# Even attention in 32-row tiles with two score sets, transposes as ordinary matmuls, out panels beside the head norm, rotation inside the projections

## The chip, the cores and the metric

The kernel runs on one core of one Trainium2 chip. The metric is the device time of one execution in microseconds (us); the median of the timed runs counts. PE is the matmul engine, DVE the vector engine, ACT the scalar engine, POOL the general one, SP the engine that issues most DMAs.

## The reference

Two model blocks over 512 tokens of width 1024 (and 256 context tokens), all in float32. The change touches the first mixer of the first block, the even one:

```
px, pc = hx @ w_in, hc @ w_in                    # x and context, 8 parts of 512 columns
qa, ka = axial_rope(q part), axial_rope(k part)  # x tokens only; 8 heads, 2 maps each, 32 wide
s = einsum(q, k) * 32**-0.5                      # per head and map m = 0, 1
p = softmax(s); a = p[m=0] - lam * p[m=1]        # lam = exp(..) - exp(..) + lam_init
o = einsum(a, v)                                 # v 64 wide
out_a = rms_norm(o over the head's 64) * subln * (1 - lam_init) * silu(ga)
out_b = short_conv(bb, cb, ub) * silu(gb)
x = x + g_x * rms_norm(concat(out_a, out_b) @ w_out, norm_post)   # context alike
```

x queries see 768 keys (256 context, 512 x), context queries the 256 context keys. The odd mixer, the sliding-window attention, the SGU and two FFNs follow and are not touched.

## The kernel before

Activations lie feature-major: partitions are features, columns are tokens (TX = 512 x tokens, TC = 256 context tokens, TA = 768). Weights come in panels of 128x2048 through a ring of three slots. A panel is loaded by SP (`load`, which waits until the panel three before has been used), split by DVE (`split_at`) into a rounded high part `whi` and the rest `wlo` (which takes the place of `raw`), and used by PE in three fast passes per product, high x high, high x low, low x high (`mm3`). So a "512-column pass" is one such matmul instruction. Products written in plain float32 run as two instructions each.

Even projections are panels 0 to 15 (`even_panel`). Panels 0 to 3 give q and k, 4 and 5 v (token-major), 6 and 7 the gate, 8 to 15 the conv branch, for which DVE forms z (`zed`) and the gated result (`b_free`). After most panels PE also does a modulation product for the next layer (`mod_panel`, 32-column tiles) and turns its row into columns (`mod_columns`).

Then `rot` is multiplied into q and k in eight steps of 512 columns (one per 128 features), and DVE applies cosine and sine in three passes a step (L1549 to L1551). The order of work on each engine is the order of the program; engines meet only at semaphores.

Even attention has 48 units (head h, query tile t): t = 0 to 3 are x tiles (768 keys, "long"), t = 4, 5 context tiles (256 keys, "short"). Per unit:
- PE: scores of both maps (`stacked_product`, L525 and L526). The stationary operand holds the query's high part in one half of its rows and the low part in the other, the moving operand the key twice, so that K = 128 and two passes do. ACT makes the high parts and copies them (`even_hi`), POOL the low parts (`lo_part`, L1873).
- DVE: a maximum for each map (L1566). ACT: an exponential for each with its row sum (L1011). Each map has one pair of PSUM banks.
- DVE: 1/sum, product with -lambda (L1579), scaling (L1581), sum of the two maps (L1582).
- PE: six (two) 128x128 transposes into banks 4 and 5 (L474). ACT: one copy.
- PE: PV of the head before, in four parts (L563, L567), banks 6 and 7.

After the last unit: squares, sums over each head's 64 features (48 matmuls of 2 columns, L592), root, reciprocal (`hwide`), spread over the features by matmuls with the identity (L601), product with the gated heads, split into high and low parts (`mixed`, counted 1 to 8 in the order in which the out panels need them). Out panels `out0` 0 to 3 follow: the first paced by `mixed`, the others whole. ACT squares and copies each panel's result before its banks are used again.

Of the kernel before, what the change touches and what calls it, by code (L numbers as in the profile page):

```python
# [34 lines left out]
P = 128  # L35
# [53 lines left out]
def build_kernel(nc, dram, out):  # L89
    with ExitStack() as ctx:  # L90
# [35 lines left out]
        hroot = nc.alloc_sbuf_tensor_at("hroot", [P, 4, 6, 2], F32, offset=temp_at + 4 * 1600)  # L126
# [17 lines left out]
        def par(name, i, n=1):  # L144
# [8 lines left out]
        hwide = place("hwide", A0, [4, 6, P])  # L153
# [11 lines left out]
        atc = [place(f"atc{i}", 6144 + i * 512, [2, 256]) for i in range(2)]  # L165
        prob = [place(f"prob{i}", 7168 + i * 1536, [2, TA]) for i in range(3)]
# [67 lines left out]
                                            "copied", "pv", "out", "zeroed", "hi", "lo", "sq", "sums", "root", "inverse", "spread",  # L234
                                            "normed", "mixed", "lam", "lam_exp")}
# [15 lines left out]

        block = ctx.enter_context(nc.Block())
# [3 lines left out]
        def mod_bank(layer, k):  # L256

            return ps[:, 5 if layer == 0 and k < 8 else 7, 0:256]
# [3 lines left out]
        def _(sp):  # L262
# [53 lines left out]
        def _(pe):  # L316
# [3 lines left out]
            def mm3(o, lhi, llo, rhi, rlo, first, last):  # L320
                pe.matmul(o, r(lhi), r(rhi), start=first, stop=False)  # L321
                pe.matmul(o, r(lhi), r(rlo), start=False, stop=False)  # L322
                return pe.matmul(o, r(llo), r(rhi), start=False, stop=last)  # L323
# [8 lines left out]
            def ctx_part(n, bank, j, kt, hi, lo, first, last):  # L332
                return mm3(ps[:, bank, j * TC:(j + 1) * TC], w(n, 0, kt, at=j * P), w(n, 1, kt, at=j * P),
                           hi[:, kt, TX:TA], lo[:, kt, TX:TA], first, last)
# [176 lines left out]
            for e in range(2, 16):  # L511
                even_panel(e)
                if e in MOD1_AFTER:
                    m = MOD1_AFTER.index(e)
                    if m == 1:
                        pe.wait_ge(mod_ready, 4)
                    if m:
                        mod_columns(1, m - 1)
                    mod_panel(1, m)
            mod_columns(1, 11)  # L520
# [9 lines left out]
            pe.wait_ge(b_free, 4)  # L530
            for t in range(8):
                if t >= 2:
                    pe.wait_ge(rot_done, t - 1)
                src = (eq, ek)[t // 4]
                pe.matmul(ps[:, t % 2, :], rot, src[:, t % 4, 0:TX], start=True, stop=True).then_inc(rot_mm, 1)
            pe.wait_ge(rot_done, 8)


            units = [(h, t) for h in range(A_HEADS) for t in range(6)]

            def even_scores(v):
                h, t = units[v // 2]
                m, b = v % 2, 2 * (v % 2)
                if v % 12 == 0:
                    pe.wait_ge(ea["lo"], 3 * (h + 1))
                if v >= 2:
                    pe.wait_ge(ea["exp"], v - 1)
                if t < 4:
                    stacked_product(ps[:, b, :], ESTK[h % 2], m * TA + t * P, TA, 0, TX)
                    last = stacked_product(ps[:, b + 1, 0:TC], ESTK[h % 2], m * TA + t * P, TA, TX, TC)  # L550
                else:
                    last = stacked_product(ps[:, b, 0:TC], ESTK[h % 2], m * TA + t * P, TA, TX, TC)
                last.then_inc(ea["scores"], 1)

            def even_pv(h, part):

                if part == 0:
                    pe.wait_ge(ea["copied"], 6 * h + 6)
                    if h >= 1:
                        pe.wait_ge(ea["out"], h)  # L560
                if part < 3:
                    for kt in range(2 * part, 2 * part + 2):
# [1484 lines left out]
```

## Time and profile before

| What | us |
|---|---|
| timed runs, median (lowest, highest) | 2592.1 (2591.42, 2594.13) |
| profiled execution, time | 2594.67 |
| profiled execution, span | 2592.9 |
| PE busy in the span | 2352.1 (91%) |
| DVE, ACT, POOL busy | 1461.0, 609.2, 132.9 |
| mean granted clock of TensorE | 0.942 |
| first scores of even attention start at | 404.27 |

Times of rows are us from the start of the span. An engine's busy time is summed over its instructions, overlaps counted once. A matmul's duration contains its way through the array, so consecutive ones overlap in the rows: the distance between two starts is what each costs. In the windows the sixth figure is the granted clock, a share of 2.4 GHz (0.50 is 1.2 GHz). A group's idle time is put down to what ended it.

### The profile page before, as it was taken

To read this page: it belongs to the slowest core of one execution; us is meant where nothing else is said; L and a number is where in the kernel's file an instruction comes from. 1 tells how busy PE (TensorE), PEld (TensorE's weight loads), DVE (VectorE), ACT (ScalarE), POOL (GpSimd) and SP (SyncE) were. 2 spreads that over 40 slices of the span, in tenths; PEclk is the share of its full clock that TensorE was granted. 3 is DMA by queue.
4 is the path that set the end of the run, shared out by engine and by line. 5 is a ranking of instruction groups with operands and counts; after the bars stand their busy time and mean duration, and the time that the engine had idled before them with its cause. 6 is when DMAs were issued, how large, how long until landed. Compare 5 with 4: busy or idle time off the path is not lost.

```text
span 2592.9 us, 28152 instructions
## 1 busy us (share of the span) xinstructions
PE 2352.1 (91%) x11796; PEld 1896.6 (73%) x11796; DVE 1461.0 (56%) x1764; ACT 609.2 (23%) x1138; POOL 132.9 (5%) x81
## 2 busy tenths in 40 slices
PE   6999985778999988897788999998999999999997
PEld 5788864444887954476467888888988787788886
DVE  2222356786455128663966877435468834787733
ACT  2111005664122127323732111002110100211100
POOL 0000002120000014003100000000000000000000
PEclk9899996888989999998799999998999999999999
DMA  8022320000112111111021222231222223122232
GB/s 329 17 98 98 130 81 1 1 1 33 49 38 77 65 54 34 56 51 64 1 81 66 98 98 88 89 115 67 82 82 82 82 85 110 65 98 98 83 101 77
DMA packets 30701, 195.97 MB, mean 76 GB/s; under 512 B 3440, under 2 KB 3696, under 8 KB 12528
## 3 DMA queue, kind: packets, MB, share of 16 engines
q1 hardware_dynamic: 29136, 188.03, 20.0%
q10 hardware_dynamic: 1440, 6.16, 0.7%
q8 instruction: 93, 1.52, 0.2%
q14 instruction: 32, 0.26, 0.0%
HBM read 192.08 MB, written 2.10 MB: 75 GB/s over the span
## 4 chain that ended last, share of the span: by engine, by line
PE 80%; DVE 14%; ACT 3%; issue 1%; DMA 1%; POOL 1%; DVEq 0%; SPq 0%; ACTq 0%; POOLq 0%
PE ps L321 20%; PE ps L322 19%; PE ps L323 19%; PE ps L377 3%; PE ps L379 3%; PE ps L378 3%; PE ps L430 2%; PE ps L563 2%; PE ps L474 2%; DVE stat L1566 1%; PE ps L712 1%; PE ps L525 1%; PE ps L689 1%; PE ps L414 1%; DVE prob L1582 1%
## 5 line engine op out<-in xcount | busy, mean ns | idle before, releaser
L1363 DVE CAST whi<-raw 128x2048 fp32r<-128x2048 f32 (+2 forms) x162 | 183.8, 1135 | 541.9 <-DMA raw<-in_even 145.2
L321 PE MATMUL ps<-h2hi,whi 128*128 128x512 f32 x1040 | 409.3, 394 | 18.3 <-DVE h2lo L1460 12.1
L322 PE MATMUL ps<-h2lo,whi 128*128 128x512 f32 x1040 | 407.0, 391 | 0.0
L323 PE MATMUL ps<-h2hi,wlo 128*128 128x512 f32 x1040 | 406.7, 391 | 0.0
L1364 DVE TENSOR_TENSOR wlo<-raw,whi 128x2048 fp32r<-128x2048 f32 (+2 forms) x162 | 341.6, 2108 | 5.6
L321 PE MATMUL ps<-h1hi,whi 128*128 128x512 f32 (+1 forms) x768 | 272.0, 354 | 16.2 <-DVE h1lo L1405 8.1
L322 PE MATMUL ps<-h1lo,whi 128*128 128x512 f32 (+1 forms) x768 | 270.1, 352 | 0.0
L323 PE MATMUL ps<-h1hi,wlo 128*128 128x512 f32 (+1 forms) x768 | 268.1, 349 | 0.0
L321 PEld LDWEIGHTS ps<-h2hi,whi 128*128 128x128 f32 x1040 | 196.8, 189 | 61.0 <-issue 13.8
L323 PEld LDWEIGHTS ps<-h2hi,wlo 128*128 128x128 f32 x1040 | 196.6, 189 | 41.2
L322 PEld LDWEIGHTS ps<-h2lo,whi 128*128 128x128 f32 x1040 | 196.8, 189 | 40.5
L321 PE MATMUL ps<-mhi,whi 128*128 128x512 f32 x544 | 213.0, 392 | 6.6 <-DVE mlo L1383 3.9
L322 PE MATMUL ps<-mlo,whi 128*128 128x512 f32 x544 | 212.6, 391 | 0.0
L323 PE MATMUL ps<-mhi,wlo 128*128 128x512 f32 x544 | 212.6, 391 | 0.0
L525 PE MATMUL ps<-wlo,whi 128*128 128x256 f32 (+2 forms) x288 | 115.3, 408 | 70.8 <-POOL wlo L1873 30.3
L321 PEld LDWEIGHTS ps<-h1hi,whi 128*128 128x128 f32 x768 | 147.6, 192 | 42.5 <-issue 17.8
L525 PEld LDWEIGHTS ps<-wlo,whi 128*128 128x128 f32 x288 | 63.6, 221 | 136.7 <-issue 60.6
L323 PEld LDWEIGHTS ps<-h1hi,wlo 128*128 128x128 f32 x768 | 146.7, 191 | 20.0
L322 PEld LDWEIGHTS ps<-h1lo,whi 128*128 128x128 f32 x768 | 147.5, 192 | 18.2
L889 ACT ACTIVATE temp<-ps 128x512 f32<-128x512 f32 (+1 forms) x48 | 25.4, 564 | 448.7 <-PE ps L323 448.7
L377 PE MATMUL ps<-whi,h2hi 128*128 128x256 f32 x416 | 119.9, 288 | 7.7 <-DVE h2lo L1460 4.0
L321 PEld LDWEIGHTS ps<-mhi,whi 128*128 128x128 f32 x544 | 102.8, 189 | 29.2 <-issue 4.3
(245 smaller groups left out, 3661.1 us busy)
## 6 DMA issues: line engine op xcount, KB each, us to landing
raw<-in_ffn_in SPq DMA_DIRECT2D x44, 1024.0 KB, 4.8
raw<-in_ffn_out SPq DMA_DIRECT2D x32, 704.0 KB, 4.0
raw<-in_even SPq DMA_DIRECT2D x16, 1024.0 KB, 6.9
mod_w<-in_mod SPq DMA_DIRECT2D x6, 2048.0 KB, 25.9
mraw<-in_mod SPq DMA_DIRECT2D x12, 1024.0 KB, 4.9
raw<-in_odd SPq DMA_DIRECT2D x12, 1024.0 KB, 4.8
raw<-in_sgu_v SPq DMA_DIRECT2D x12, 1024.0 KB, 4.8
raw<-in_sgu_u SPq DMA_DIRECT2D x12, 1024.0 KB, 4.9
```

The lines of the kernel that those rows point to most:

```text
L321: pe.matmul(o, r(lhi), r(rhi), start=first, stop=False)
L322: pe.matmul(o, r(lhi), r(rlo), start=False, stop=False)
L323: return pe.matmul(o, r(llo), r(rhi), start=False, stop=last)
L377: pe.matmul(o, lhi, rhi, start=first, stop=False, **kw)
L378: pe.matmul(o, lhi, rlo, start=False, stop=False, **kw)
L379: return pe.matmul(o, llo, rhi, start=False, stop=last, **kw)
L430: done = pe.matmul(ps[:, 6, 48 + t:49 + t], tile[:, t * P:(t + 1) * P], ones[:, 0:1], start=first and t == tiles[0], stop=last, skip_group ...
L474: return pe.transpose(o, in_, ident)
L525: pe.matmul(o, q, r(wlo[:, slot, k_at:k_at + n]), start=True, stop=False)
L563: pe.matmul(ps[0:64, 6, :], ev[:, kt, h * 64:h * 64 + 64], atx[h % 2][:, kt, :], start=kt == 0, stop=kt == 5)
L1363: step(dve.tensor_copy(whi[:, slot, 0:width].bitcast(F32R), raw[:, slot, 0:width]))
L1364: tell(dve.tensor_tensor(wlo[:, slot, 0:width].bitcast(F32R), raw[:, slot, 0:width], whi[:, slot, 0:width], ALU.subtract), split_done, n + 1)
```

## The change

- **Rotation in the projections.** One rotation (bank 7) goes in front of each of panels 4 to 11, and DVE's `rope(n)` between its splits. Order q0, k0, q1, k1, ... The modulation banks move to bank 6.
- **Scores in 32-row tiles.** q and k keep all features of two heads in one 128-partition tile; each map's 32 features are one row tile. Three passes (high-high, high-low, low-high) with K = 32. The low parts `eql`, `ekl` are made by DVE; POOL has no part left, and no zeroing is needed. Units are (head pair hp, tile t, head a).
- **Two score sets.** Unit u uses banks 0 to 2 or 3 to 5, both maps in 1536 consecutive columns. DVE takes both maxima in one instruction, the probabilities in one pass less (ratio of the sums times -lambda), and leaves the division by the first sum to the head norm: `stat[:, 32:80]` keeps it, and 64 eps sum^2 is added to the sum of squares.
- **Transposes** are plain float32 matmuls with the identity as moving operand, all in bank 6: four chunks, copy, two chunks, copy.
- **PV** per pair of heads and query tile, one head in each half of the columns, bank 7.
- **Head norm and out panels.** The squares of earlier pairs are made inside attention, in `esq`. Out panels 0 and 1 are computed together, one input tile at a time (`out0_pair`), between the sums and spreads. Their banks are 0 to 5. The panels' loads are released at scores 24 and 48 of 48.

The diff's core follows; removed beside it are POOL's loop over the even heads' low parts, DVE's zeroing, and the serial rope loop. `rope(4 + 2 * j)` stands right after the z product that tells `zed`.

```diff
@@ sync
-                        sp.wait_ge(ea["scores"], 96)
+                        sp.wait_ge(ea["scores"], 24)
+                    elif (phase, k) == ("out0", 2):
+                        sp.wait_ge(ea["scores"], 48)
@@ tensor
             for e in range(2, 16):
+                if 4 <= e < 12:
+                    side, j = ROPE[e - 4]
+                    pe.wait_ge(e_free, 2 * side + j // 2 + 1)
+                    if e > 4:
+                        pe.wait_ge(rot_done, e - 4)
+                    pe.matmul(ps[:, 7, :], rot, (eq, ek)[side][:, j, 0:TX], start=True, stop=True).then_inc(rot_mm, 1)
                 even_panel(e)
+            def even_scores(u):
+                hp, t, a = EVEN_UNITS[u]
+                b, slot, at = 3 * (u % 2), ESTK[hp // 2], hp % 2 * TA
+                if t == 0 and a == 0:
+                    pe.wait_ge(ea["lo"], 2 * (hp + 1))
+                if u >= 2:
+                    pe.wait_ge(ea["exp"], 2 * (u - 1))
+                def term(o, m, i, k0, n):
+                    rows = slice(64 * a + 32 * m, 64 * a + 32 * m + 32)
+                    q = (whi[rows, slot, at + t * P:at + t * P + P], eql[rows, hp, t * P:(t + 1) * P])[i == 2]
+                    k = (wlo[rows, slot, at + k0:at + k0 + n], ekl[rows, hp, k0:k0 + n])[i == 1]
+                    return pe.matmul(o, r(q), r(k), start=i == 0, stop=i == 2)
+                if t < 4:
+                    for i in range(3):
+                        first = term(ps[:, b + 1, 0:256], 0, i, 512, 256)
+                    first.then_inc(ea["bank_shared"], 1)
+                    for i in range(3):
+                        term(ps[:, b, :], 0, i, 0, 512)
+                        term(ps[:, b + 2, :], 1, i, 256, 512)
+                    pe.wait_ge(ea["bank_shared"], 8 * hp + 2 * t + a + 1)
+                    for i in range(3):
+                        last = term(ps[:, b + 1, 256:512], 1, i, 0, 256)
+                else:
+                    for i in range(3):
+                        for m in range(2):
+                            last = term(ps[:, b + m, 0:256], m, i, 512, 256)
+                last.then_inc(ea["scores"], 1)
+            for u, (hp, t, a) in enumerate(EVEN_UNITS):
+                if u + 2 < len(EVEN_UNITS):
+                    even_scores(u + 2)
+                pe.wait_ge(ea["probs"], u + 1)
+                if t < 4:
+                    even_transposes(u, range(4), moved[u])
+                if u >= 2:
+                    even_pv(u // 2 - 1, u % 2)
+                even_transposes(u, range(4, 6), moved[u] + (t < 4))
...
+            for t in range(3):
+                head_sums(t)
+            out0_pair(0)
+            head_sums(3)
+            out0_pair(1)
+            pe.wait_ge(ea["out"], 8)
+            for t in range(4):
+                head_spread(t)
+                out0_pair(2 + t)
+            out0_pair(6)
+            out0_pair(7)
@@ scalar
+            for u, (hp, t, a) in enumerate(EVEN_UNITS):
+                if u + 1 < len(EVEN_UNITS):
+                    even_exp(u + 1)
+                even_copy(u)
+                if (t, a) == (1, 0) and hp < 3:
+                    even_hi(hp + 1)
+                if (t, a) == (0, 1) and hp:
+                    even_out(hp - 1, 1)
+                    even_square(hp - 1)
+                elif (t, a) == (4, 1):
+                    even_out(hp, 0)
@@ vector
             for n in range(4, 9):
+                if n >= 6:
+                    rope(n - 6)
                 split_at(n)
             for j in range(4):
+                if j < 3:
+                    rope(3 + 2 * j)
                 split_at(9 + 2 * j)
...
+                if j < 2:
+                    rope(4 + 2 * j)
...
+            for u, (hp, t, a) in enumerate(EVEN_UNITS):
+                n = TA if t < 4 else TC
+                i = u % 4
+                dve.wait_ge(ea["exp"], 2 * u + 2)
+                step(dve.reciprocal(stat[:, 12 + i:13 + i], stat[:, 8 + i:9 + i]))
+                step(dve.scalar_tensor_tensor(out=stat[:, 16 + i:17 + i], in0=stat[:, 32 + u:33 + u], scalar=lam4[:, 3:4],
+                                              in1=stat[:, 12 + i:13 + i], op0=ALU.mult, op1=ALU.mult))
+                p = prob[u % 3]
+                dve.scalar_tensor_tensor(out=p[:, 0, 0:n], in0=p[:, 1, 0:n], scalar=stat[:, 16 + i:17 + i],
+                                         in1=p[:, 0, 0:n], op0=ALU.mult, op1=ALU.add).then_inc(ea["probs"], 1)
+                if u + 2 < len(EVEN_UNITS):
+                    even_max(u + 2)
+                if (t, a) == (2, 0) and hp < 3:
+                    even_lo(hp + 1)
+                if (t, a) == (2, 1) and hp:
+                    gated_head(hp - 1)
+                if (t, a) == (4, 1):
+                    split_tensor(h1hi, h1lo, np.s_[:, 4 + hp, :], eob[:, hp, :], ea["mixed"], hp + 1)
+                if u in (20, 37):
+                    split_at(FIRST["out0"] + (u == 37))
```

`out0_pair(i)` waits for `mixed` i + 1 (the first also for the second panel's split and the last exponential) and does the four x and context parts of both panels for input tile i. `head_spread(t)` waits for `inverse` t + 1 and, from the second on, for the product of the tile before.

## Rows read from the trace of the kernel before

**Rows 1.** Windows by stage: length, then busy us and count by engine, clock, DMA.
```profile
371.67:404.27 32.60, 13.25 (x16) 3.59 (x17) 22.08 (x36) 6.93 (x9) 6.54 (x5) 0.66 0.14 57
404.27:625.23 220.96, 171.65 (x648) 104.96 (x648) 179.09 (x290) 128.87 (x274) 39.10 (x21) 0.81 0.02 9
625.23:656.56 31.33, 25.23 (x121) 19.64 (x121) 17.30 (x24) 7.54 (x12) 0.00 (x0) 0.78 0.02 9
656.56:690.40 33.84, 33.84 (x196) 29.68 (x195) 16.73 (x15) 3.16 (x6) 0.00 (x0) 1.00 0.09 32
```

**Rows 2.** DVE groups by form, even attention: count, busy us, mean ns, idle before.
```profile
L1566 DVE TENSOR_REDUCE stat<-ps 128x1 f32<-128x768 f32 x64 | 58.7, 953 | 30.3 <-PE ps L526 29.9
L1582 DVE SCALAR_TENSOR_TENSOR prob<-prob,stat 128x768 f32<-128x768 f32 x24 | 32.9, 1373 | 0.8
...
L1579 DVE TENSOR_TENSOR stat<-stat,lam 128x1 f32<-128x1 f32 x48 | 17.0, 354 | 1.7
L1566 DVE TENSOR_REDUCE stat<-ps 128x1 f32<-128x256 f32 x32 | 12.1, 418 | 15.2 <-PE ps L526 14.9
L1582 DVE SCALAR_TENSOR_TENSOR temp<-temp,stat 128x768 f32<-128x768 f32 x8 | 8.1, 1018 | 0.3
L1578 DVE RECIPROCAL stat<-stat 128x2 f32<-128x2 f32 x48 | 7.4, 155 | 0.1
```

**Rows 3.** ACT groups by form, even attention.
```profile
L1011 ACT ACTIVATE prob<-ps,stat 128x768 f32<-128x768 f32 x48 | 42.9, 897 | 42.3 <-DVE stat L1566 42.0
L889 ACT ACTIVATE atx<-ps 128x768 f32<-128x768 f32 x32 | 25.8, 807 | 2.4 <-PE ps L474 1.5
```

**Rows 4.** Timeline of PE, one long unit: start, us, what.
```profile
512.42 0.39 PE L526 MATMUL ps<-wlo,whi 128*128 128x512 f32 x1
512.65 0.28 PE L525 MATMUL ps<-wlo,whi 128*128 128x256 f32 x1
...
513.60 0.82 PE L474 MATMUL ps<-mats,prob 128*128 128x128 f32 x6
514.34 1.93 PE L563 MATMUL ps<-atx,ev 128*64 128x512 f32 x4
516.20 0.50 PE L525 MATMUL ps<-wlo,whi 128*128 128x512 f32 x1
```

**Rows 5.** Timeline of PE, head norm.
```profile
636.49 9.09 PE L592 MATMUL ps<-mats,temp 128*128 128x2 f32 x48 [1.96 <-ACT temp L889]
...
652.65 1.58 PE L601 MATMUL ps<-mats,hwide 128*128 128x128 f32 x12 [0.46 <-DVE ega L1603]
```

**Rows 6.** Timeline at the ends of panels 8 and 9, and of one rope pass.
```profile
240.18 1.07 PE L414 MATMUL ps<-mraw,cs 128*32 128x256 f32 x16
...
241.52 0.69 DVE L1519 TENSOR_TENSOR zpad<-eob,ps 128x512 f32<-128x512 f32 x1
...
258.51 1.07 PE L414 MATMUL ps<-mraw,cs 128*32 128x256 f32 x16
...
261.03 0.69 DVE L1531 TENSOR_TENSOR eob<-sgb,ycv 128x512 f32<-128x512 f32 x1
...
377.50 0.69 DVE L1550 TENSOR_TENSOR eq<-eq,wave 128x512 f32<-128x512 f32 x1
```

**Rows 7.** Windows after a thin stretch, and in odd attention.
```profile
109.80:115.40 5.60, 5.60 (x19) 4.73 (x19) 0.67 (x4) 0.00 (x0) 0.00 (x0) 0.50 0.01 1
1016.00:1056.00 40.00, 34.35 (x151) 18.89 (x150) 31.86 (x47) 27.42 (x46) 14.68 (x9) 1.00 0.08 25
```

**Rows 8.** Timeline of DVE and ACT: first and last probabilities, panel 0's copies.
```profile
416.63 1.02 DVE L1582 SCALAR_TENSOR_TENSOR prob<-prob,stat 128x768 f32<-128x768 f32 x1
...
624.75 0.48 DVE L1582 SCALAR_TENSOR_TENSOR temp<-temp,stat 128x256 f32<-128x256 f32 x1
...
673.69 1.64 ACT L889 ACTIVATE temp<-ps 128x512 f32<-128x512 f32 x4 [27.77 <-PE ps L323]
...
675.85 1.03 ACT L889 ACTIVATE y<-ps 128x1024 f32<-128x1024 f32 x1
```

More of the change, by code:

```diff
@@ L164, in build_kernel @@
         atx = [place(f"atx{i}", i * 3072, [6, 512]) for i in range(2)]
[L165 to L166 removed]
+        ept = [place(f"ept{i}", i * 768, [6, P]) for i in range(4)]
+        prob = [place(f"prob{i}", 6144 + i * 1536, [2, TA]) for i in range(2)]
         prob.append(temp[:, 0:2 * TA].rearrange("p (m n) -> p m n", m=2))
@@ L250, in build_kernel @@
                                            "rowsum", "ws", "rows_copied", "uhalf")}
+        EVEN_UNITS = [(hp, t, a) for hp in range(4) for t in range(6) for a in range(2)]
+        EVEN_MOVES = [2 if t < 4 else 1 for _, t, _ in EVEN_UNITS]
+        moved = [sum(EVEN_MOVES[:u]) for u in range(len(EVEN_UNITS) + 1)]
+        ROPE = [(side, j) for j in range(4) for side in range(2)]
         block = ctx.enter_context(nc.Block())
@@ new lines, in even_pv @@
+            def even_pv(p, half):
+                hp, t, _ = EVEN_UNITS[2 * p]
+                kts = (range(3 * half, 3 * half + 3), range(4 + half, 5 + half))[t >= 4]
+                if half == 0:
+                    pe.wait_ge(ea["copied"], moved[2 * p + 2])
+                    if t == 4:
+                        pe.wait_ge(ea["out"], 2 * hp + 1)
+                    elif t == 0 and hp:
+                        pe.wait_ge(ea["out"], 2 * hp)
+                for kt in kts:
+                    for a in range(2):
+                        h = 2 * hp + a
+                        last = pe.matmul(ps[64 * a:64 * a + 64, 7, t % 4 * P:t % 4 * P + P], ev[:, kt, h * 64:h * 64 + 64],
+                                         ept[(2 * p + a) % 4][:, kt, :], start=kt == (0 if t < 4 else 4), stop=kt == 5)
+                if half:
+                    last.then_inc(ea["pv"], 1)
@@ new lines, in even_transposes @@
+            def even_transposes(u, kts, n):
+                if n:
+                    pe.wait_ge(ea["copied"], n)
+                for i, kt in enumerate(kts):
+                    at = kt * P if EVEN_UNITS[u][1] < 4 else (kt - 4) * P
+                    last = pe.matmul(ps[:, 6, i * P:(i + 1) * P], prob[u % 3][:, 0, at:at + P], ident,
+                                     start=True, stop=True)
+                last.then_inc(ea["transposed"], 1)
+            pe.wait_ge(b_free, 4)
+            even_scores(0)
@@ L603, in _, with out0_pair @@
                                      start=True, stop=True)
                 last.then_inc(ea["spread"], 1)
+            p0 = FIRST["out0"]
+            kts0 = (4, 5, 6, 7, 0, 1, 2, 3)
+            def out0_pair(i):
+                kt = kts0[i]
+                if i == 0:
+                    pe.wait_ge(split_done, p0 + 2)
+                    pe.wait_ge(ea["exp"], 96)
+                pe.wait_ge(ea["mixed"], i + 1)
+                for k in range(2):
+                    for j in range(2):
+                        x_part(p0 + k, 2 * k + j, j, kt, h1hi, h1lo, i == 0, i == KT - 1)
+                        last = ctx_part(p0 + k, 4 + k, j, kt, h1hi, h1lo, i == 0 and j == 0, i == KT - 1,
+                                        skip_group_check=True)
+                    if i == KT - 1:
+                        last.then_inc(panel_done, 1)
@@ L1073, in out_copy @@
+            act.preload_act_table(ACT.Sqrt)
+            even_out(3, 1)
+            even_square(3)
+            act.wait_ge(ea["var"], 1)
+            tell(copy(stat[:, 32:80], stat[:, 32:80], ACT.Sqrt, scale=1.0 / 64), ea["root"], 1)
             def out_copy(phase, norm, dst, bias=None):
```

319 lines of the change are left out of this document (108 added, 211 removed).

## The prediction

> **What bounds it now.** The profiled execution spans 2592.9 us and took 2594.67 us; the three timed runs have their median at 2592.1 us. The sum below is made against 2594.67, and the difference of 2.6 us is taken off at the end. Over the whole span PE is busy 91% on the page, which says little about the part that changes. So I cut the span by stage first [rows 1]. In the 32.6 us between the last gate product and the first scores PE works 13.25 us and DVE 22.08: rotation, zeroing and the high and low parts run one after another. In the 221 us of even attention PE is busy 171.65 us at a granted clock of 0.81, DVE 179.09 and ACT 128.87: no engine is full. In the next 31.3 us (head norm) PE does nothing but small products, and only then come 33.8 us of full-clock panels.
>
> Next the groups inside attention [rows 2]. The 48 products by lambda over 1/sum, 128x1, average 354 ns, and the sum of the two probability sets takes 1373 ns when written to prob but 1018 when written to temp. The first of these is the same instruction on the same shape. In the trace the long ones lie under POOL's low parts (39.10 us of POOL in this stage [rows 1]). The stage is thus a loop of DVE, ACT and PE waiting for one another, slowed by POOL's work on DVE's operands. The marks that I use below are the end of the first probability tile (417.65), the end of the 48th (625.23), and the end of the second out0 panel (690.40) [rows 1, 8].
>
> **Start of attention.** Before, 371.67 to 417.65 is 46.0 us. The eight rotations go in front of panels 4 to 11. Each is a full fp32 product of 512 columns, two instructions; four such take 516.20 - 514.34 = 1.86 us [rows 4], so one costs 0.93, and PE is full there: 8 x 0.93 = 7.4 us. A second cost stands in the order of queues. Bank 7 is single, so rotation n+1 waits for DVE's rope(n). rope(4) stands behind zed(1), and that behind panel 8; rope(5) stands behind the gate products of panel 9; rope(6) behind zed(2). After panel 8 DVE finishes the z product at 241.52 + 0.69 = 242.21 and then needs three 0.69 passes with their gaps, 2.2 us, to 244.4; PE is through with its modulation product at 241.25. That is a wait of 3.1 us. After panel 9 the gate products end at 261.72 and the rope at 263.9, with PE free at 259.58: 4.3 us. After panel 10 again 3.1. Together 10.5 us [rows 6]. All other ropes are done during a panel, under its 17 us of PE work. After idle or thin stretches the clock has been at 0.50, also with full matmuls running: 5.6 us at 0.50 with PE wholly busy [rows 7]. I charge 5 us for three such waits (0 if it does not fall, 8 if all three cost the half of 5.6 us).
>
> What then follows the last gate product: scores 1.6, maximum 1.8, two exponentials 1.9, probabilities 1.4 (each derived below), 6.7 us. Zeroing, eight serial ropes (8 x 2.2), ACT's and POOL's parts are gone or lie under panels 12 to 15, where DVE idles most of the time. Sum: 7.4 + 10.5 + 5 + 6.7 = 29.6 against 46.0: **gain 16.4**. If the projections had no cover, rope alone would cost its 17.6 us again.
>
> **One long unit (t < 4).** PE: a high-precision 512-column pass runs at a pitch of 0.23 and a 256-column one, taken as half, at 0.12 [rows 4]. The new scores have 4608 columns a unit: 3 x 0.12, three pairs of 512, 3 x 0.12. No 32-row tile stands in this trace. The nearest row is the modulation product in 32-column tiles: 16 instructions that alone would need 16 x 0.21 = 3.4 us take 1.07 [rows 6]; tiles of the array do overlap. I take the pairs as overlapping: 0.36 + 0.69 + 0.36 = 1.41, with a change of tile 1.6. Not overlapping: 2.1 and 2.3. Transposes as ordinary fp32 matmuls are the same instruction as the spread of the head norm, 12 in 1.58 us [rows 5], against 0.74 for six transposes (513.60 to 514.34 [rows 4]). Eight of them 1.1, four 0.65 (1.75 for six: dearer by 1.0 a unit). PV has the same columns as before, 128 wide in two 64-column tiles: half a pair is 12 instructions of 0.107, in six overlapping steps 0.64, with change of tile 0.8; serial 1.4. Before, it was 6.6 us a head, 1.1 a unit. PE sum 1.6 + 1.1 + 0.8 + 0.65 = **4.15**.
>
> DVE: the maximum costs 953 ns for 768 and 418 for 256 elements [rows 2], so 1.76 for 1536 and 0.69 for 512. Reciprocal 0.155, the product as much (both are 128x1), sum 1.02: 3.15 with gaps. ACT: 2 x 0.9 + copy in two pieces (0.81 for one piece, and a second start) 1.0 = 2.8 [rows 3]; in a loop with the wait for the second transposes, because bank 6 is one, 1.8 + 0.6 + 0.7 + 0.4 = 3.5. So PE is last, T = 4.15, and both others have 0.6 us or more of room.
>
> **One short unit (t = 4, 5).** Six 256-column passes 0.5, two transposes 0.65, PV 0.35: 1.5; but the chain exp, probabilities 0.9, PV, transposes, is 1.9 to 2.0. I take 2.0.
>
> **What else sits in the loop.** even_lo 3 x 2.0, two panel splits of 3.6 us, four split_tensor of 1.6, three gated_head of 1.0 on DVE; on ACT even_hi 3 x 1.7, outputs and squares. A split at u = 20 and 37 makes the probabilities about 2.5 us late each, the four split_tensor 1.2 each in short units, the rest 2: 12 us. Four short stretches with thin PE work let the clock fall for a while: 6 us (0 to 16). From the first to the last probability tile: 31 x 4.15 + 16 x 2.0 + 12 + 6 = 179 us against 207.6: **gain 28.5**.
>
> **End.** Before, 690.40 - 625.23 = 65.2. After: last transposes, copy and PV 1.6; 48 small sum products took 9.09 us [rows 5] in a stage whose clock averages 0.78 [rows 1], so 5 to 9, taken 6.5; 16 quarter pairs at full clock are the 33.4 us of panels 0 and 1 [rows 1]; four spreads 4 x 1.58 = 6.3; a thin start 2. PE is then busy throughout: 49.8. DVE needs 2.6 us a head tile, well under a pair plus a spread (5.7). New is a wait before panel 2: both panels end together, ACT needs 673.69 to 676.88 = 3.2 us for one of them [rows 8], and panel 0 ends only 2.1 us before panel 1: 1.1. The load of the fourth panel, released 16 us later than before, has the 17 us of panel 2 as cover. Sum 50.9: **gain 14.3**.
>
> Together 16.4 + 28.5 + 14.3 = 59.2: 2594.67 - 59.2 = 2535.5, on the level of the timed runs 2533.
>
> **Two rules that bear on it.** 40 us of odd attention run with the same transposes at PE 34.35 us busy and clock 1.00 throughout [rows 7]; so by the row transposes as such do not hold the clock down. The Trainium skill ("TensorE: Matmul & The Clock Gate", PE-mode transpose) says that transpose mode does not count as PE activity for the clock. By the rule the ordinary matmuls would buy the clock back, by the row the density does, and my sum has full clock either way.
> The change of tile shows in the row as 1.86 for PV where four passes of 0.43 are 1.72: 0.14 us [rows 4]. The Trainium skill ("TensorEngine Tiling (Array Packing)", Key Properties) says that changing the tiling mode drains the engine; the rival below prices that.
>
> **Rivals.**
> *The tiles do not overlap.* PE in order, as [rows 4] show for full tiles. Scores +0.69 a long and +0.35 a short unit, 27 us: 2560. PV serial as well, +0.65 and +0.2, 23 us: 2583. For it: the operands share read paths; against it the 1.07 us of [rows 6].
> *Dear tile changes.* Four a unit instead of two. At 0.4 us in place of 0.14 it is 0.25 x 4 x 47 = 47 us: 2580. This is what the rule on draining would do. These two together 0.22.
> *The clock stays low (the other side).* PE's 161 us of units scale with it. At 0.81 (as now) +38: 2571. At 0.50, +161: 2694, slower. It decides at 161/(161 + 59) = 0.73. For it: 32 or 64 of the array's 128 rows work in a score pass, and thin stretches stand in every head pair; against it: the clock of 1.00 in odd attention. Slower 0.06, the middle case is in the range.
> *ACT or the single transposes bank binds, PE cheaper than thought.* T = 3.5: -20 us: 2513. 0.10.
> *No effect:* the loop waits so long on bank 6 (both copies, 1.0 us with latencies and no PE cover) that T is 6.0, 1.9 x 31 = 59 us more. Then 2592: 0.02.
> My forecast 0.60, its own range 2515 to 2556.
>
> **Range.** 2505 (no clock loss, ACT loop) to 2583 (serial tiles). Over 0.2% (about what a measurement here tells from nothing, 5 us) faster 0.92, within 0.02, slower 0.06.
>
> **What would show it.** PE between 417 and 625 at clock near 1.00, one long unit at 4.15 us from maximum to maximum; two score instructions of a pair starting within 0.05 us; the reduce at 1.76 us; L1579's successor at 0.16 instead of 0.354; waits of PE for the rope of 3 to 4 us before panels 9, 10, 11; the first score 17 us or more after 371.7; PE full from the last PV to the end of panel 1. Wrong if PE waits for ACT's copies each unit, if pairs start 0.23 us apart, or if the clock in the stage is under 0.85.

## The result, and the profile after

The changed kernel takes 2553.1 us (median of four runs, 2549.2 to 2556.6), the kernel before 2593.1 beside it (2591.4 to 2595.7). The ratio is 0.9844, with a 95% interval of 0.9825 to 0.9863: 40 us faster. The forecast was 59 us faster, 2533. The profiled execution took 2550.83 us against 2594.67, with a span of 2549.1 us, and the following goes by it: 43.8 us gained.

The three marks that the prediction used split this. First the windows by stage of the changed kernel, with the columns of [rows 1]: from the last gate product to the end of the first probabilities, from there to the end of the 48th, and on to the end of the second out0 panel. Then come stretches of the second stage.

```profile
386.86:393.87 7.01, 4.29 (x37) 4.03 (x39) 5.41 (x9) 3.64 (x8) 1.09 (x1) 0.68 0.69 273
393.87:591.66 197.79, 173.97 (x1330) 142.87 (x1326) 138.60 (x210) 114.23 (x278) 0.00 (x0) 0.82 0.04 12
591.66:645.76 54.10, 53.57 (x306) 47.62 (x305) 17.18 (x22) 5.53 (x11) 0.00 (x0) 0.85 0.02 4
393.00:410.00 17.00, 15.63 (x79) 13.57 (x75) 10.05 (x13) 6.95 (x15) 0.00 (x0) 0.51 0.01 1
410.00:475.00 65.00, 56.56 (x526) 46.02 (x522) 49.31 (x76) 44.90 (x107) 0.00 (x0) 1.00 0.00 1
475.00:502.00 27.00, 23.60 (x135) 19.15 (x134) 19.61 (x28) 11.72 (x32) 0.00 (x0) 0.62 0.12 40
545.00:580.00 35.00, 31.59 (x177) 26.64 (x177) 21.09 (x27) 15.58 (x35) 0.00 (x0) 0.57 0.00 1
```

| part | before | after | gain | forecast gain |
|---|---|---|---|---|
| start of the span to first probabilities | 417.65 | 393.87 | 23.8 | 16.4 |
| first to 48th probabilities | 207.6 | 197.8 | 9.8 | 28.5 |
| from there to the third panel's first product | 65.2 | 54.1 + 1.2 | 9.9 | 14.3 |

Two parts gave less than forecast, one gave more. The large miss is attention, and the last four rows show where to look: for 65 us the clock is 1.00 throughout, but over three stretches it averages 0.51, 0.62 and 0.57, which is mostly time at 0.50 (1.2 GHz). PE is busy 87 to 92% of each, and 87% of the full-clock stretch too, so the busy share doesn't tell them apart.

What the units cost is seen in DVE's groups by form, which answer to [rows 2] (count, busy us, mean ns, idle before):

```profile
L1614 DVE TENSOR_REDUCE stat<-ps 128x2 f32<-128x1536 f32 x30 | 52.7, 1756 | 37.6 <-PE ps L556 37.6
L1632 DVE SCALAR_TENSOR_TENSOR prob<-prob,stat 128x768 f32<-128x768 f32 x24 | 24.4, 1019 | 0.8
L1614 DVE TENSOR_REDUCE stat<-ps 128x2 f32<-128x512 f32 x16 | 11.0, 689 | 12.5 <-PE ps L556 12.5
L1629 DVE SCALAR_TENSOR_TENSOR stat<-stat,lam 128x1 f32<-128x1 f32 x47 | 10.3, 220 | 1.7
```

The maxima are the forecast 1.76 and 0.69 us. With POOL's 39 us gone from the stage, the sum to prob falls from 1373 to 1019 ns, and the product from 354 to 220 ns (forecast 155). Both means before hide two kinds of row. Six of the 24 sums took 2.43 or 2.44 us, each while POOL was at work, and the other 18 took 1.02:

```profile
440.39 1.99 POOL L1873 TENSOR_TENSOR wlo<-ek,wlo 64x768 fp32r<-64x768 f32 x1
440.76 2.44 DVE L1582 SCALAR_TENSOR_TENSOR prob<-prob,stat 128x768 f32<-128x768 f32 x1
```

The products before were 0.16 us, but for six of 1.65 to 1.79 us under POOL's work. So the new product, another instruction, is dearer than the usual old one (0.22 for 0.16); only the six long ones are gone. DVE's idle time in front of the long maxima, 37.6 us, is all put down to PE's scores. But PE waits too, 23 us in the stage, 16 of them for DVE's probabilities and 7 for ACT's copies: PE is last in most units, not in all.

PE's timeline answers to [rows 4]: start, us, what. The first lines are a unit at clock 1.00, the later ones two units at 0.50.

```profile
448.89 0.51 PE L556 MATMUL ps<-wlo,whi 32*128 32x256 f32 x2
449.11 0.28 PE L556 MATMUL ps<-ekl,whi 32*128 32x256 f32 x1
449.23 0.28 PE L556 MATMUL ps<-wlo,eql 32*128 32x256 f32 x1
449.24 0.40 PE L556 MATMUL ps<-ekl,whi 32*128 32x512 f32 x1
...
450.17 1.16 PE L598 MATMUL ps<-mats,temp 128*128 128x128 f32 x8
451.25 0.88 PE L587 MATMUL ps<-ept,ev 128*64 128x128 f32 x12
452.83 0.71 PE L598 MATMUL ps<-mats,temp 128*128 128x128 f32 x4 [0.70 <-ACT ept L942]
...
551.24 2.08 PE L598 MATMUL ps<-mats,temp 128*128 128x128 f32 x8 [3.03 <-DVE temp L1632]
...
558.11 2.08 PE L598 MATMUL ps<-mats,prob 128*128 128x128 f32 x8
560.11 1.55 PE L587 MATMUL ps<-ept,ev 128*64 128x128 f32 x12
561.59 1.22 PE L598 MATMUL ps<-mats,prob 128*128 128x128 f32 x4
562.74 0.81 PE L556 MATMUL ps<-wlo,whi 32*128 32x256 f32 x2
...
564.97 2.08 PE L598 MATMUL ps<-mats,prob 128*128 128x128 f32 x8
```

Passes for the two 32-row tiles start 0.01 us apart (449.23 and 449.24), so they overlap. At full clock a unit is 1.28 us of scores (448.89 to 450.17), 1.08 of transposes, 0.80 of PV and 0.65 of transposes: 3.8 us, 0.35 less than forecast. Waits fill that up, here 0.70 for ACT's copy. At 0.50 nothing waits, and the unit from 558.11 to 564.97 takes 6.86 us, 2.7 us more than the forecast 4.15.

Ahead of the low stretch stands the wait of 3.03 us at 551.24. DVE's timeline says what it is made of: the two instructions of the split at u = 37.

```profile
544.46 1.76 DVE L1614 TENSOR_REDUCE stat<-ps 128x2 f32<-128x1536 f32 x1 [2.14 <-PE ps L556]
546.13 1.22 DVE L1404 CAST whi<-raw 128x2048 fp32r<-128x2048 f32 x1
547.38 2.29 DVE L1405 TENSOR_TENSOR wlo<-raw,whi 128x2048 fp32r<-128x2048 f32 x1
549.71 0.16 DVE L1628 RECIPROCAL stat<-stat 128x1 f32<-128x1 f32 x1
```

The split at u = 20 makes a like wait, 3.14 us before 480.33, and the clock falls there too. Is it the cause, or does the clock fall anyway?

### The profile page after: what moved, and what is told of

Its sections match the earlier page's. It is cut to its first block, busy times and chain, and to the rows that moved or that the text cites. A ratio compares the mean times of both kernels' runs of the same rounds, so it can differ in the third digit from the quotient of the medians.

```text
span 2549.1 us, 29355 instructions
## 1 busy us (share of the span) xinstructions
PE 2345.8 (92%) x12500; PEld 1936.2 (76%) x12500; DVE 1409.3 (55%) x1673; ACT 589.3 (23%) x1138; POOL 88.0 (3%) x57
## 4 chain that ended last, share of the span: by engine, by line
PE 83%; DVE 11%; ACT 2%; issue 1%; DMA 1%; POOL 1%; SPq 0%; DVEq 0%; ACTq 0%; POOLq 0%
PE ps L329 20%; PE ps L330 20%; PE ps L331 20%; PE ps L385 3%; PE ps L386 3%; PE ps L387 3%; PE ps L598 2%; PE ps L438 2%; PE ps L556 1%; PE ps L765 1%; PE ps L742 1%; DVE stat L1614 1%; PE ps L482 1%; PE ps L918 1%; PE ps L587 1%
## 5 line engine op out<-in xcount | busy, mean ns | idle before, releaser
L386 PE MATMUL ps<-wlo,h2hi 128*128 128x256 f32 x416 | 119.4, 287 | 0.0
L387 PE MATMUL ps<-whi,h2lo 128*128 128x256 f32 x416 | 119.3, 287 | 0.0
```

Of the source, the lines that this page charges most:

```text
L386: pe.matmul(o, lhi, rlo, start=False, stop=False, **kw)
L387: return pe.matmul(o, llo, rhi, start=False, stop=last, **kw)
```

## Experiments

Times are medians of four runs unless another count is given, ratios are against the kernel before on the same chip. Its median there was 2592.5 to 2594.3, so differences of 2 us between experiments say nothing.

**Both splits out of the loop**

```
-                if u in (20, 37):
-                    split_at(FIRST["out0"] + (u == 37))
+            split_at(FIRST["out0"])        # after the loop over u
+            split_at(FIRST["out0"] + 1)
```

> DVE's two panel splits leave the attention loop and stand behind the 48th unit, where DVE idles for the head sums. Theory A (a wait of PE of 3 us drops the clock to 0.50, and the loop, once at 0.50, stays there for 20 to 30 us): with the two waits (3.1 and 3.0 us) gone, the low stretches 475 to 502 and 545 to 580 go too; first to last probability tile 197.8 becomes about 178 (5 us of waits, some 15 us of clock), total 2553 becomes about 2535. Rival B (the low stretches come anyway, from the thin short units or the 32-row passes): only the waits go, about 5 us, 2548, and the clock in the loop stays at 0.82.

2532.9 us (2531.7 to 2537.4), ratio 0.9774 [0.9758, 0.9791]: 20 us less than the changed kernel. The stage from first to last probabilities:

```profile
399.34:574.41 175.07, 155.92 (x1329) 127.15 (x1325) 131.74 (x206) 114.12 (x278) 0.00 (x0) 0.92 0.04 13
```

175.1 us for 197.8, and clock 0.92 for 0.82. The two waits are 6.2 us together, so most of the 22.7 us is more than the waits themselves. That is theory A; what is left at 0.50 is mostly the start of the stage.

**The waits filled, the splits where they were**

```
+                if u in (21, 38):
+                    pe.wait_ge(ea["copied"], moved[u])
+                    for _ in range(4):
+                        pe.matmul(ps[:, 6, :], blk, wave[:, 0, :], start=True, stop=True)
                 pe.wait_ge(ea["probs"], u + 1)
```

> The changed kernel, DVE's two panel splits stay where they are, but PE works on four dummy float32 matmuls (3.7 us) in each of the two waits behind them. Theory A (the wait costs mainly by the clock): waits stay, the stretches at 0.50 behind them go, some 15 us: 2536 to 2542. Rival B (run 1 gained by the freed 7 us of DVE): no gain, 2553 or slower.

2538.7 us (2536.3 to 2539.6), ratio 0.9784 [0.9769, 0.9799]: 14 us less, with 2 x 3.7 us of useless products put into PE's queue and DVE's splits as late as before. The windows over the stretches that were low:

```profile
475.00:505.00 30.00, 27.39 (x229) 20.43 (x229) 24.52 (x38) 18.60 (x48) 0.00 (x0) 1.00 0.11 37
505.00:570.00 65.00, 59.30 (x514) 47.16 (x515) 52.20 (x77) 42.81 (x103) 0.00 (x0) 0.97 0.00 1
```

Each against the kernel before beside it, late splits gain 59.6 us, filled waits 55.6 and the changed kernel 40.0. So some 16 of the 20 us come back with DVE as late as before, by the clock alone. The rest, 4 to 6 us, is about the length of the two waits; the two ratios' intervals overlap, so it isn't told from nothing. Nor does this run say whether the missing wait or the dense full-array work put in its place held the clock.

**The start of the stage kept busy**

```
+            def warm(n):
+                for _ in range(n):
+                    pe.matmul(ps[:, 7, :], r(whi[:, 15 % RING, 0:P]), r(h1hi[:, 0, 0:TX]), start=True, stop=True)
+            pe.wait_ge(rot_done, 8)
+            warm(12)
             pe.wait_ge(b_free, 4)
...
             mod_columns(1, 11)
+            warm(12)
             pe.wait_ge(mod_ready, 6)
```

> 24 dummy full-array passes (128x512, no result is read), 12 while PE waits for the last gate product and 12 while it waits for the modulation. The time of the changed kernel is 2553. Theory A (the long stretch at 0.50 at the start of attention comes from these two idle gaps of 2.1 and 2.7 us and the thin work around them): the stretch 390 to 410 runs at 1.00, 4 units at 4.2 in place of 6.1 us, total about 2545. Rival B (the stretch comes from the start of the loop itself, where PE waits for the first exponentials): no change, or 1 us slower.

2543.2 us (2542.2 to 2549.9), ratio 0.9811 [0.979, 0.9831]: 10 us less. The 17 us that stood at 0.51 after the last gate product now show:

```profile
390.85:398.61 7.76, 7.54 (x56) 5.87 (x54) 5.42 (x11) 3.64 (x8) 1.09 (x1) 1.00 0.64 247
398.61:415.00 16.39, 13.93 (x121) 11.76 (x122) 12.31 (x17) 11.52 (x25) 0.00 (x0) 1.00 0.00 1
```

So the gaps there did bring the low stretch (theory A). But the whole stage took 182.8 us here for 197.8, 15 us less, and 17 us at full clock instead of 0.51 are worth only 6 or 7. The rest comes from the second split, which this edit doesn't touch. PE waits 3.02 us behind it as in the changed kernel, and yet the clock is back within some 5 us. The same holds nearly in the profile of the next experiment, with a wait of 3.03. The windows from about that split on, in this one and the next:

```profile
545.00:580.00 35.00, 28.75 (x261) 23.39 (x259) 27.11 (x41) 21.74 (x56) 0.00 (x0) 0.95 0.06 19
548.00:583.00 35.00, 28.96 (x253) 23.67 (x250) 25.20 (x42) 20.86 (x54) 0.00 (x0) 0.90 0.08 26
```

The changed kernel's profile had 0.57 over the same 35 us. Five profiles have both splits in the loop with open waits, ordinary matmuls and overlapping row tiles: the changed kernel, this one, the next, the one with the passes in another order and the one with the panels after the norm. Behind the split at u = 20 the clock stays low for 20 to 45 us in all five; behind the one at u = 37 it does so in the changed kernel's alone (0.90 to 0.95 over 35 us in the other four, for waits of 2.7 to 3.0 us). A wait of 3 us is followed by a fall each time, but how long it lasts is not the wait's doing alone.

**Ropes ahead of the products that hold them up**

```
             for j in range(4):
-                if j < 3:
-                    rope(3 + 2 * j)
+                if j == 0:
+                    rope(3)
                 split_at(9 + 2 * j)
+                if j < 2:
+                    rope(4 + 2 * j)
...
-                if j < 2:
-                    rope(4 + 2 * j)
...
+                if j < 2:
+                    rope(5 + 2 * j)
                 dve.wait_ge(sg_in, j + 1)
```

> rope(4) to rope(7) are moved ahead of the z and gate products that they waited behind. Theory A: PE's three waits of 3.3, 4.5 and 3.3 us go, and the three drops of clock behind them (240 to 250, 260 to 270, 290 to 300 at 0.83) with them: 11 us plus 3 to 5, total about 2538. Rival B: the panels lean on DMA or on DVE elsewhere, and the wait appears at the next split: 0 to 5 us.

2534.0 us (2531.1 to 2543.5), ratio 0.9781 [0.976, 0.9802]: 19 us less. In the changed kernel the waits of PE from 240 to 300 us hold this (us in total, times, longest):

```profile
PE ps L525 <- DVE eq L1561: 6.6, 2, 3.3
PE ps L525 <- DVE ek L1561: 4.5, 1, 4.5
```

11.1 us against 10.5 forecast. In this experiment they are gone, PE is full through the stretch, and the last gate product comes at 376.38 for 386.86. That 10.5 us equals the forecast only by chance, since panel 2 ended 5.0 us later in this execution: from there to the last gate product it is 15.5 us less, the 11.1 of waits and 4.4 of clock. Its windows:

```profile
240.00:310.00 70.00, 70.00 (x437) 58.49 (x437) 30.02 (x34) 5.45 (x12) 0.00 (x0) 1.00 0.32 121
380.00:425.00 45.00, 41.86 (x212) 35.95 (x214) 24.95 (x36) 21.70 (x47) 0.21 (x1) 0.50 0.02 9
```

The profiled execution was the longest of the four, 2543.5 us, and its clock was at 0.50 for 45 us of attention (PE busy 93%). That its three other runs are up to 12 us shorter would fit a clock that came back sooner there, but they have no trace.

**All three edits together**

> Late splits, early ropes and the dummy passes together. If each removes its own gap: 20 + 19 less the overlap, and the start of attention at full clock: 2505 to 2512. If the clock only moves its low stretch elsewhere: 2515 to 2525.

2513.3 us (2506.1 to 2515.9), ratio 0.9682 [0.9663, 0.9702]. The stage is

```profile
383.21:551.94 168.73, 148.49 (x1323) 120.90 (x1324) 131.61 (x206) 114.38 (x278) 0.00 (x0) 0.97 0.04 14
```

The forecast for attention less its 6 us of clock and 5 of splits was 168. The time lies 1 us outside theory A's range and short of theory B's; with the clock at 0.97 the edits add up nearly as A says (40 us under the changed kernel, for 20 + 19 + 10 less what they share).

**Transposes back in transpose mode: in the changed kernel, and in the one with the three edits**

```
-                    last = pe.matmul(ps[:, 6, i * P:(i + 1) * P], prob[u % 3][:, 0, at:at + P], ident, start=True, stop=True)
+                    last = transposed(ps[:, 6, i * P:(i + 1) * P], prob[u % 3][:, 0, at:at + P])
```

> The new loop with PE's transpose mode in place of the ordinary matmuls, nothing else. Theory A (clock is set by how full PE is, the kind of transpose does not matter): PE saves about 0.8 us in each long unit (0.74 in place of 1.7 for six), 25 us at most, total 2535 to 2545. Rival B (transpose mode does not count for the clock): the loop falls to 0.50 more often and stays there, clock of the stage under 0.75, total 2560 or more.

> The same with PE's transpose mode. Run 3 had the clock of the stage at 0.62 with it, at 7 us less than the changed kernel. Theory A (transpose mode brings the clock down whatever stands around it): low stretches remain, slower than the three edits alone by 5 to 20 us. Rival B (the low stretches were started by the gaps alone): clock near 1.00 and, with 0.8 us less for PE in each long unit, up to 15 us faster than the three edits alone.

In the changed kernel: 2546.4 us (2541.9 to 2554.1), ratio 0.9826 [0.9808, 0.9844], 7 us less than with ordinary matmuls, but the ratio's interval overlaps that of the changed kernel (0.9825 to 0.9863). On top of the three edits: 2530.0 us (2520.9 to 2530.9), ratio 0.9744 [0.9723, 0.9764], 17 us more. The stage in the one and the other:

```profile
397.78:586.69 188.91, 172.67 (x1108) 126.84 (x1104) 138.15 (x209) 114.25 (x279) 0.00 (x0) 0.62 0.04 12
```

```profile
383.13:564.36 181.23, 165.91 (x1102) 121.25 (x1102) 130.76 (x206) 114.44 (x279) 0.00 (x0) 0.66 0.04 13
```

With them the clock is 0.62 and 0.66. In the changed kernel that is the clock of rival B with almost the time of theory A. The edit saves PE work and costs the clock; in the changed kernel the two about cancel, and where the clock was at 0.97 the loss of 17 us is clear.

**Ordinary matmuls alone, in the kernel before**

```
-                    last = transposed(ps[:, 4 + kt // 4, kt % 4 * P:kt % 4 * P + P],
-                                      prob[u % 4][:, 0, kt * P:(kt + 1) * P])
+                    last = pe.matmul(ps[:, 4 + kt // 4, kt % 4 * P:kt % 4 * P + P],
+                                     prob[u % 4][:, 0, kt * P:(kt + 1) * P], ident, start=True, stop=True)
```

> The kernel before the change with one part of the change alone: its even attention transposes are ordinary matmuls. PE pays 0.8 us more in a long unit, 30 us in all if PE were last there. Theory A (ordinary matmuls hold the clock up): the stage's clock goes from 0.81 to 0.90 or more and the time stays within 10 us of 2593, or falls. Rival B (kind of transpose does not matter for the clock in that loop): 10 to 25 us slower.

2602.2 us (ten runs, 2597.0 to 2609.2) beside 2594.3: ratio 1.0029 [1.002, 1.0039], 8 us more. The stage of this kernel, and then of the kernel before between the same marks:

```profile
415.08:626.86 211.78, 171.41 (x834) 120.40 (x834) 171.50 (x280) 123.61 (x262) 33.73 (x18) 0.91 0.02 9
```

```profile
417.65:625.23 207.58, 160.72 (x619) 96.36 (x618) 171.48 (x281) 122.92 (x262) 33.72 (x18) 0.83 0.03 9
```

The clock rises, and PE is still busy 10.7 us longer; the stage loses 4.2. Here transpose mode is the better one, by 8 us, so the choice does have both signs. That ordinary matmuls also give PE more work to do is a rival that no run separates from the kind of transpose.

**Order of the passes, then no overlap of the row tiles at all**

```
-                    for i in range(3):
-                        term(ps[:, b, :], 0, i, 0, 512)
-                        term(ps[:, b + 2, :], 1, i, 256, 512)
+                    for m in range(2):
+                        for i in range(3):
+                            term(ps[:, b + 2 * m, :], m, i, 256 * m, 512)
...
-                    for i in range(3):
-                        for m in range(2):
+                    for m in range(2):
+                        for i in range(3):
                             last = term(ps[:, b + m, 0:256], m, i, 512, 256)
```

> The same score passes with each map's three together, so that neighbours in the queue are always in the same row tile. If the overlap of row tiles is what keeps scores at 1.27 us a unit, a long unit costs 3 x 0.115 x 2 = 0.69 us more and a short one 0.35, 27 us in all at full clock: 2575 to 2585. If the order does not matter (the queue finds the pairs itself, or PE is not last), under 5 us.

2558.4 us (2554.7 to 2562.2), ratio 0.9869 [0.9855, 0.9884], 5 us more; the ratio's interval overlaps that of the changed kernel, so this is not told from nothing. PE's timeline shows why so little:

```profile
446.35 0.28 PE L556 MATMUL ps<-wlo,eql 32*128 32x256 f32 x1
446.36 0.51 PE L556 MATMUL ps<-wlo,whi 32*128 32x512 f32 x2
446.69 0.39 PE L556 MATMUL ps<-ekl,whi 32*128 32x512 f32 x1
```

The `x2` holds two 512-column passes within 0.51 us: a pass for the second tile starts beside the first tile's, though three of the first stand ahead of it in the queue. What the order did lose is the overlap at the ends: this unit's scores take 1.59 us (446.01 to 447.60) for 1.28, and waits elsewhere hide most of it. The order did not separate the long passes, so a second kernel did it with a wait (`bank_shared` is raised after the first map's passes, and the second map's wait for it):

```
                     for i in range(3):
-                        first = term(ps[:, b + 1, 0:256], 0, i, 512, 256)
+                        term(ps[:, b + 1, 0:256], 0, i, 512, 256)
+                    for i in range(3):
+                        first = term(ps[:, b, :], 0, i, 0, 512)
                     first.then_inc(ea["bank_shared"], 1)
+                    pe.wait_ge(ea["bank_shared"], 8 * hp + 2 * t + a + 1)
                     for i in range(3):
-                        term(ps[:, b, :], 0, i, 0, 512)
                         term(ps[:, b + 2, :], 1, i, 256, 512)
-                    pe.wait_ge(ea["bank_shared"], 8 * hp + 2 * t + a + 1)
```

> The changed kernel, with the second map's long passes held back until the first map's are finished, so that no two row tiles work at once. Run 4 changed only the order and its passes still overlapped. If overlap is worth its passes: 0.69 us and one semaphore, 0.8 to 0.9 us in each of 32 long units, 26 to 29 us at full clock less what the loop hides: 2570 to 2585. If PE is not last in the loop: under 8 us.

2631.4 us (2630.7 to 2634.2), ratio 1.0145 [1.013, 1.016]: 78 us more, and slower than the kernel before. Both expectations had it too low. The whole stage, and a stretch of it:

```profile
400.60:669.20 268.60, 258.93 (x1332) 195.67 (x1331) 139.13 (x209) 114.15 (x280) 0.00 (x0) 0.66 0.03 9
...
460.00:490.00 30.00, 29.53 (x98) 21.64 (x100) 11.96 (x18) 10.94 (x25) 0.00 (x0) 0.50 0.00 1
```

PE is busy 29.53 of 30 us, and the clock is 0.50. Two long maxima stand 8.53 us apart there (479.38 and 487.91 in DVE's timeline), against 6.87 at 0.50 in the changed kernel. That is 1.66 us a unit, so by estimate half, 0.83, at full clock, and 31 x 0.83 = 26 us for the lost overlap with its semaphore. The other 50 or so go with the clock, 0.66 for 0.82; this too is an estimate, since no run has the overlap lost at full clock. The rival "tiles do not overlap" was priced at 27 us without this.

**Panels after the whole head norm**

All sums and spreads first, then `out0_pair(0)` to `out0_pair(7)`:

```
-            for t in range(3):
+            for t in range(4):
                 head_sums(t)
-            out0_pair(0)
-            head_sums(3)
-            out0_pair(1)
             pe.wait_ge(ea["out"], 8)
+            pe.wait_ge(ea["exp"], 96)
             for t in range(4):
                 head_spread(t)
-                out0_pair(2 + t)
-            out0_pair(6)
-            out0_pair(7)
+            for i in range(8):
+                out0_pair(i)
```

> In the changed kernel all sums and spreads of the head norm come before the first pair of out panels, as before the change. The forecast put the gain of the interleaving at 14 us, the trace shows 10 from the last probabilities to the third panel. If PE full without gaps is the cause, this run is 8 to 12 us slower (2561 to 2565); if the pairs only fill time that the clock gives back at 0.50, under 5.

2561.3 us (2555.0 to 2565.5), ratio 0.987 [0.985, 0.989]: 8 us more. The end stage up to the second panel's last product:

```profile
589.95:654.48 64.53, 58.50 (x304) 52.31 (x304) 17.17 (x23) 5.48 (x11) 0.00 (x0) 0.76 0.02 4
```

64.5 us against 54.1: laying the first panels beside the norm is worth 10.4 us to this mark in these two profiles, of the 14 forecast for the whole end. About half is gaps (PE idles 6.0 us for 0.5), the other half a lower clock (0.76 for 0.85, PE busy 4.9 us longer).

**The three edits, with the last two waits filled as well**

```
+                if u >= 46:
+                    for _ in range(u - 45):
+                        pe.matmul(ps[:, 2, :], blk, wave[:, 0, :], start=True, stop=True)
                 pe.wait_ge(ea["probs"], u + 1)
```

> The three edits of run 6 and three dummy matmuls at the last two units, where PE waits and the clock falls before the head sums. If the low stretch at the end (550 to 567 in run 6) is started by these gaps: the 36 sums take 4.2 in place of 7.8 us, transposes and first pair 2 to 3 us less, total 5 us under run 6 (about 2508). If the sums themselves (2 columns each) bring the clock down: no change, or 1 us slower.

2512.2 us (2511.0 to 2517.5), ratio 0.9688 [0.9672, 0.9704]: no difference to the three edits that these runs can tell. The 36 sums took 5.96 us for 7.84, but the clock still left 1.00; with the three edits alone these 20 us had 0.57:

```profile
550.00:570.00 20.00, 18.55 (x105) 14.95 (x104) 10.80 (x14) 5.29 (x12) 0.00 (x0) 0.83 0.12 49
```

## Why the prediction was right, and where it was off

- **Start, 23.8 gained for 16.4.** The steps held: 7.0 us from the last gate product to the first probabilities (6.7 forecast), 11.1 us of waits for ropes (10.5). From the end of panel 2 to the last gate product the kernel before took 242.1 us and the changed one 262.6, which is 20.5 more against 22.9 for rotations, waits and clock. With the ropes early it took 247.1: waits and their clock are the forecast 15.5, the rest 5.0 for the 7.4 put down for rotations. The other 5.3 us of the difference lie ahead of all that the change touches: panel 2 ended at 124.28 for 129.56. They belong to the execution, not to the change: in the eleven other profiles with the change it ended 3 to 5 us later, and in one without it 3.4 us later. Without this luck the start gains 18.5.
- **Attention, 9.8 for 28.5: here the forecast failed.** The overlap and the maxima were right. So was the length of a unit, but partly by luck: the seven maxima from 439.36 to 464.56, in the full-clock stretch, stand 3.1 to 4.9 us apart, 4.2 in the mean, of which PE works 3.8 and waits the rest. The mis-sized term is the sentence "Four short stretches with thin PE work let the clock fall for a while: 6 us (0 to 16)". The windows show 17 us at 0.51, 27 at 0.62 and 35 at 0.57, some 68 us at 0.50 together; where a unit takes 6.87 for 4.2, they cost by estimate 68 x 0.39 = 27 us. The price of the splits, "about 2.5 us late each", is near the 3.1 us of wait, but the wait is the small part: filling both gives 14 to 16 us back, moving the splits 20. Keeping PE busy at the start gives 10, of which the start's own stretch explains 6 or 7. The prediction's own sign of being wrong, a clock under 0.85 in the stage, was met at 0.82; the time stayed inside the range because the clock term, though four times too small, was one of several.
- **Why it was mis-sized.** The forecast took from [rows 7] that density alone keeps the clock up, and that a fall lasts as long as the 5.6 us seen there. Neither carries over. At 0.50 this loop stayed down 20 to 45 us with PE 87 to 93% busy. And the kind of transposes counts: three comparisons (0.82 and 0.62, 0.97 and 0.66, and 0.91 and 0.83 in the kernel before) have the lower clock with transpose mode. The Trainium skill ("TensorE: Matmul & The Clock Gate", PE-mode transpose) says that this mode does not count as PE activity for the clock; these runs agree that the clock is lower with it, while odd attention, at 1.00 with the same mode [rows 7], shows that the mode alone doesn't hold the clock down. By the row as I read it the choice made no difference; it makes 17 us once the gaps are gone.
- **End, 9.9 for 14.3.** The wait before panel 2 was 1.23 us (1.1 forecast), PE was full. In the end stage PE's timeline shows the terms:

```profile
594.37 1.12 PE L587 MATMUL ps<-ept,ev 128*64 128x128 f32 x8 [0.53 <-ACT ept L942]
595.42 7.84 PE L623 MATMUL ps<-mats,esq 128*128 128x2 f32 x36
...
609.52 1.40 PE L623 MATMUL ps<-mats,esq 128*128 128x2 f32 x12
...
646.99 0.50 PE L329 MATMUL ps<-h1hi,whi 128*128 128x512 f32 x1 [1.23 <-ACT y L942]
```

  Sums of 7.84 and 1.40 are 9.2, at the top of "5 to 9, taken 6.5". The clock makes the difference: over the 36 it is 0.50 and each costs 0.22 us, over the 12 it is 1.00 and each costs 0.12. The panels behind the first 36 begin at the lower clock as well, which would be most of what else is missing.
- **The rivals.** "The tiles do not overlap" is out by the timeline. "Dear tile changes" is out: with four of them PE's work in a unit measured 3.8 us against 4.15 forecast, so none costs near 0.4 us. The Trainium skill ("TensorEngine Tiling (Array Packing)", Key Properties) has a change of tiling mode drain the engine; that may be so, but here it is worth tenths at most. "The clock stays low" happened at its middle case's clock (0.82 for 0.81), with a third of the stage at 0.50, but not at its price: 38 us and 2571 were forecast with all of PE's work stretched by the mean, and by the estimate above it cost 27. "ACT or the single transposes bank binds" is seen in waits of 0.2 to 1.0 us for the copy at full clock: 3.8 us in 65 (six waits), with 4.6 more for DVE's probabilities, which is why a cheaper PE unit brought nothing.

**Open.** The memory of the clock was seen, not explained: why odd attention keeps 1.00 with transposes where even attention does not, and why the same wait of 3.0 us is followed by 30 us at 0.50 in one profile and by some 5 in the others. Since one of the changed kernel's low stretches is not in every execution, the gains of single edits that are read from its profile hold to a few us at best. No run separates the 32-row passes' part in this from the transposes' in the changed loop.

## What to carry to other kernels

In a loop of small or partial-array products like this one, a wait of 3 us of PE is priced by what the clock does after it: look at the granted clock of the 30 us that follow, and move the intruder (here a 3.5 us split on DVE) out of the loop, or fill the wait. Edits that cost PE work but hold the clock (matmuls for transposes) have to be measured together with the removal of the gaps, since what they brought turned here: 8 us lost in the kernel before, about nothing in the changed one, 17 gained without the gaps. A mean of a group can hide two kinds of row, so look at single ones before pricing a successor. Order of DVE's queue ahead of a single bank is worth reading row by row: the waits for ropes, forecast as 3.1, 4.3 and 3.1 us, came out as 3.3, 4.5 and 3.3.

## What the hardware showed that was not expected

- With the two row tiles held apart, PE was busy 29.53 of 30 us and its clock 0.50; with them overlapped it was 1.00 in 65 us at 56.56 busy. A busy share near one says nothing of the clock: slower work fills more of the time.
- Long passes for the second 32-row tile began beside the first tile's in both orders of the queue that were run.
- Even products of 2 columns go with the clock: 0.12 us each at 1.00 (12 in 1.40 us), 0.22 at 0.50 (36 in 7.84).
- The same wait of PE (2.7 to 3.0 us, at the same place of the loop) was followed by 35 us at a mean clock of 0.57 in one profile and of 0.90 to 0.95 in four others.
